# An expert block on one core: the second half of w_down as split products, too

## What is computed

```python
gates = route(h, w_router, router_bias)            # 8 of 64 experts for each token
def per_seq(args):
    hs, gs = args
    g = jnp.einsum('sd,edf->sef', hs, w_gate)      # d = 1024, f = 256
    u = jnp.einsum('sd,edf->sef', hs, w_up)
    act = jax.nn.silu(g) * u * gs[:, :, None]
    return jnp.einsum('sef,efd->sd', act, w_down)  # the down product
```

## Time and profile before

| | us |
|---|---|
| median of 3 runs | 1070.29 |
| lowest, highest | 1069.88, 1074.86 |
| the profiled execution, device time | 1075.07 |
| the profiled execution, span of the instructions | 1073.0 |

### The profile page before, as it was taken

How to read it: one execution, slowest core, us unless ns; L and a number is a source line. 1 busy time by engine, 2 the same in 40 slices (tenths; PEclk the granted TensorE clock), 3 DMA queues, 4 the chain that set the end, 5 groups by cost and what they waited for, 6 DMA issues and landing times.

```text
span 1073.0 us, 15239 instructions
## 1 busy us (share of the span) xinstructions
PE 1019.2 (95%) x4652; PEld 743.2 (69%) x4652; DVE 870.5 (81%) x1416; ACT 644.7 (60%) x743; POOL 299.5 (28%) x224
## 2 busy tenths in 40 slices
PE   4998999999998999999999999999999999999957
PEld 0786776557754777777777777777777777777723
DVE  1669766654768899999998989999999999999785
ACT  5334135643343678777777767777777777777511
POOL 1232221440303433323322323322322332332200
PEclk9899999999999999999999999999999999999979
DMA  9667743112254799999999999999999999999993
GB/s 338 260 244 266 257 174 99 59 40 89 102 212 145 283 376 367 365 378 386 391 382 378 355 365 359 378 374 383 371 373 343 362 335 336 346 358 359 360 412 119
DMA packets 71080, 318.67 MB, mean 297 GB/s; under 512 B 17232, under 2 KB 17744, under 8 KB 44560
## 3 DMA queue, kind: packets, MB, share of 16 engines
q1 hardware_dynamic: 36816, 200.30, 49.3%
q10 hardware_dynamic: 11616, 72.66, 17.9%
q0 software_dynamic: 22624, 45.40, 11.4%
HBM read 317.25 MB, written 39.85 MB: 333 GB/s over the span
## 4 chain that ended last, share of the span: by engine, by line
PE 80%; DMA 9%; DVE 7%; ACT 2%; issue 1%; ACTq 0%; SPq 0%; POOL 0%; DVEq 0%; POOLq 0%
PE ps L1348 11%; PE ps L1350 11%; PE ps L1349 11%; PE ps L1366 10%; PE ps L1033 8%; PE ps L1372 8%; PE ps L1123 6%; DMA hg<-h_rows,idxg 6%; PE ps L1442 3%; PE ps L1225 2%; DMA yr<-y_rows 2%; PE ps L1207 2%; PE ps L1049 2%; PE ps L1174 1%; PE ps L1285 1%
## 5 line engine op out<-in xcount | busy, mean ns | idle before, releaser
L1821 DVE TENSOR_TENSOR wlo<-raw,whi 128x2048 fp32r<-128x2048 f32 x136 | 305.2, 2285 | 0.0
L891 ACT ACTIVATE whi<-raw 128x2048 fp32r<-128x2048 f32 x136 | 261.4, 1923 | 0.0
L1348 PE MATMUL ps<-whi,hthi 128*128 128x512 f32 x544 | 225.1, 414 | 0.0
L1350 PE MATMUL ps<-whi,htlo 128*128 128x512 f32 x544 | 213.8, 393 | 0.0
L1349 PE MATMUL ps<-wlo,hthi 128*128 128x512 f32 x544 | 212.5, 391 | 0.0
L661 POOL DMA_INDIRECT y_rows<-ysb,idxs x68 | 69.0, 1015 | 444.9 <-DVE idxg L1816 389.6
L934 ACT ACTIVATE ysb<-ps 128x1024 f32<-128x1024 f32 x68 | 69.6, 1024 | 175.4 <-PE ps L1372 175.4
L653 POOL DMA_INDIRECT hg<-h_rows,idxg x70 | 140.3, 2005 | 71.0 <-DVE idxg L1816 50.5
L1366 PE MATMUL ps<-rawd,actt 128*128 128x512 f32 x272 | 127.8, 592 | 2.2 <-ACT actt L927 2.2
L1350 PEld LDWEIGHTS ps<-whi,htlo 128*128 128x128 f32 x544 | 102.1, 188 | 23.0
L1349 PEld LDWEIGHTS ps<-wlo,hthi 128*128 128x128 f32 x544 | 102.9, 189 | 17.6
(11 more groups left out here) (272 smaller groups left out, 1611.7 us busy)
## 6 DMA issues: line engine op xcount, KB each, us to landing
raw<-in_w_gate_dram SPq DMA_DIRECT2D x68, 1024.0 KB, 10.9
raw<-in_w_up_dram SPq DMA_DIRECT2D x68, 1024.0 KB, 12.9
rawd<-in_w_down_dram ACTq DMA_DIRECT2D x66, 1024.0 KB, 10.1
ada<-in_w_ada_dram SPq DMA_DIRECT2D x24, 1024.0 KB, 8.3
yr<-y_rows SPq DMA_DIRECT2D x6, 2048.0 KB, 19.3
wraw<-in_w_in_dram POOLq DMA_DIRECT2D x8, 1024.0 KB, 5.7
woraw<-in_w_out_dram SPq DMA_DIRECT2D x16, 256.0 KB, 3.0
yr<-y_rows SPq DMA_DIRECT2D x8, 512.0 KB, 11.7
```

Source lines behind the costliest of these rows:

```text
L891: A(whi[:, s, m_, :], raw[:, s, m_, :], ACT.Copy).then_inc(hi_ok, 1)
L1348: mm(out_, hthi[s][:, k, :], hi, start=(k == 0), stop=False)
L1350: ins = mm(out_, htlo[s][:, k, :], hi, start=False, stop=(k == KD - 1))
L1821: V.tensor_tensor(wlo[s][:, m_, :], raw[:, s, m_, :], whi[:, s, m_, :].bitcast(F32), ALU.subtract).then_inc(lo_dve, 1)
```

## The change

The second half of the down product is split like the first. ScalarE copies the high parts of both halves, one after the other, VectorE makes both low parts, and TensorE computes both halves by three float32r products. `wdhi` now has one buffer for each half in place of one for each slot, so each block uses both. TensorE waits for `actl` and the first low part ahead of the whole down product, and no longer for `actt` and the load. `actt` is still made, since `actl` is computed from it. The one-hot rows stay on VectorE, as before. At the end, `y_out` of the last block but one moves ahead of `down_high` of the last.

```diff
             def down_high(i, s):
                 ac.wait_ge(wd_in[s], i * 16 + 16)
-                A(wdhi[s][:, :, :], rawd[:, s, :, 0:DC], ACT.Copy).then_inc(wdhi_ok, 1)
+                for hf in range(2):
+                    A(wdhi[hf][:, :, :], rawd[:, s, :, hf * DC:(hf + 1) * DC], ACT.Copy).then_inc(wdhi_ok, 1)
...
             silu(last, 1)
+            y_out(last, 0)
             down_high(last, 1)
-            y_out(last, 0)
             act_rows(last, 1)
             y_out(last, 1)
...
             def down(i, s):
-                pe.wait_ge(wd_in[s], i * 16 + 16)
-                pe.wait_ge(actt_ok, num(i, s) + 1)
+                pe.wait_ge(actl_ok, num(i, s) + 1)
                 if not (isinstance(i, int) and num(i, s) == 0):
                     pe.wait_ge(y_ok, num(i, s))
-                for k in range(KF):
-                    mm(bank(5), actt[:, k, :], rawd[:, s, k, DC:D], start=(k == 0), stop=(k == KF - 1))
-                pe.wait_ge(wdlo_ok, num(i, s) + 1)
-                pe.wait_ge(actl_ok, num(i, s) + 1)
-                for k in range(KF):
-                    for j, (a_, w) in enumerate(((acth, wdhi[s][:, k, :]), (acth, wdlo[:, s, k, 0:DC]),
-                                                 (actl, wdhi[s][:, k, :]))):
-                        ins = mm(bank(4), a_[:, k, :], w, start=(k == 0 and j == 0), stop=(k == KF - 1 and j == 2))
+                for hf in range(2):
+                    pe.wait_ge(wdlo_ok, num(i, s) * 2 + (hf + 1))
+                    for k in range(KF):
+                        hi, lo = wdhi[hf][:, k, :], wdlo[:, s, k, hf * DC:(hf + 1) * DC]
+                        mm(bank(4 + hf), acth[:, k, :], hi, start=(k == 0), stop=False)
+                        mm(bank(4 + hf), acth[:, k, :], lo, start=False, stop=False)
+                        ins = mm(bank(4 + hf), actl[:, k, :], hi, start=False, stop=(k == KF - 1))
                 ins.then_inc(dn_mm, 1)
...
             def down_low(i, s):
-                v.wait_ge(wdhi_ok, num(i, s) + 1)
-                V.tensor_tensor(wdlo[:, s, :, 0:DC], rawd[:, s, :, 0:DC], wdhi[s][:, :, :].bitcast(F32), ALU.subtract)\
-                 .then_inc(wdlo_ok, 1)
+                for hf in range(2):
+                    cols = slice(hf * DC, (hf + 1) * DC)
+                    v.wait_ge(wdhi_ok, num(i, s) * 2 + (hf + 1))
+                    V.tensor_tensor(wdlo[:, s, :, cols], rawd[:, s, :, cols], wdhi[hf][:, :, :].bitcast(F32),
+                                    ALU.subtract).then_inc(wdlo_ok, 1)
```

## The result

The changed kernel takes 1077.55 us (median of 12 runs, 1074.26 to 1083.32), the kernel before, on the same chips, 1070.88 us (12 runs, 1068.10 to 1074.86). The ratio is 1.0065, with a 95% interval from 1.0047 to 1.0083: slower by 6.7 us, where the prediction had 35.9 us.

What follows compares the result with a forecast made beforehand. TensorE bounds the kernel at 9.935 us a period; VectorE's chain, 10.48 after the change, was to take over. 65 x (10.48 - 9.935) = +35.4, tail +1.0, start -0.5: +35.9, so 1106 us, range 1095 to 1122.

Steps and rivals of the forecast that it cites:

- TensorE's part: Down product, each period: six split passes (1.40 us) replace four fp32 passes (1.72), saving 0.32; TensorE's period becomes 9.59 us.
- VectorE's added step: One more 128x1024 subtract on VectorE each period, costing 1.13 us with nothing to hide it.
- rival 3: Expert phase: the subtract is absorbed and TensorE stays the bound; 9.59 us a period, -21 us, 1049; chance 0.03.
- VectorE's own chain: VectorE's work per period before the change, two shown waits taken off: 9.35 us, becoming 10.48 with the subtract.
- Rival 2: VectorE's small gaps also close, packing it to busy time: 10.17 us a period, +15 us, 1086; chance 0.09.
- ScalarE's added copy: One more 128x1024 copy on ScalarE each period, 1.06 us, covered by its waiting ahead of `ysb`: cost 0.
- The tail: After the last w_down load: added copies and subtracts before the last down product, +1.0 us, bounds 0 and 2.3.
- Rival 1: Expert phase: TensorE and VectorE take turns and VectorE's old waits stay; 11.07 us a period, +73 us, 1144; chance 0.13.
- Rival 4: Expert phase: TensorE, idle about 0.9 us a period, loses its clock; one period in ten at 1.2 GHz, +57, 1163; chance 0.02.

Runs made afterwards that it cites:

- no_second_low: Changed kernel without VectorE's second subtract; TensorE multiplies the second half's high part twice, omitting its low part: 1075.31 us, ratio 1.0053 to the kernel before.

## Why the prediction was right and wrong

**TensorE's part** was right: six more split passes for four fp32 ones; its own work fell from 9.91 to about 9.54 (from the load at 710.51 to the next ready at 720.15 in the rows above, less 0.10 of waiting for `actl`), and its waits moved to `actl` and the second `wlo`, as forecast.

**VectorE's added step** was right at 1.13 us (1.14), and so was rival 3's rejection: nothing hides it, and a third one costs the same again.

**The failed term is VectorE's own chain**, taken as 9.35 us and worth 8.9. I took the two waits shown in the earlier trace rows off the period and called the rest work. Idle time is counted from the end of the instruction before, but an instruction with nothing to wait for starts before that end: `vcur` 0.09 us before the end of `wdlo` in the earlier trace rows, `actl` 0.09 before the end of the one-hot rows in the changed kernel. A wait shorter than that overlap can't show at all, and a longer one is shown short. The chain held three such waits: `actl` for `acth` (0.29), `slotv` for the indices (0.11), `htlo` for `hthi` (0.03 to 0.05). The 0.29 went unseen in three parts: 0.09 of overlap, 0.15 by which the fourth one-hot record was longer, and the 0.05 from its end (705.23 + 0.89) to 706.17, to which the profile gives no mark. That largest wait stood in my own rows: ScalarE ends `acth` at 706.14 and VectorE starts `actl` at 706.17. I used the 706.14 to argue that `acth` would not be late, and did not compare it with the 706.17. 0.44 us in 65 periods is 29 us, and that is the error of the sum: 35.9 - 28.6 = 7.3, measured 6.7. Rival 2 had the right sign for another reason (closing the gaps in which VectorE reads its own results back); those stayed, as `slotv` to `destr`, 0.31 us, shows. Nor was its 10.17 us a floor: the period came out at 10.04. The busy time of 9.04 contained the longer record of the fourth one-hot instruction (0.15 us), and with the waits gone records overlap that did not before (0.13 us at `slotv`, 0.09 at `actl`). So my sign for rival 2, a period under 10.3, would have named it wrongly.

**ScalarE's added copy at cost 0** was true only beside a VectorE that is as late. `no_second_low` shows it: with VectorE relieved the period is 9.98, not 9.59, and VectorE waits for `acth`, behind that copy. What the copy costs by itself was not measured. I had looked at ScalarE's share and at its one deadline. The loop that it closes spans two blocks: down product, `ysb`, `hthi`, the copies, `acth`, `actl`, both low parts, and back to TensorE. Added up from the rows of `no_second_low` it is 9.9 us a block, and a share of 82% does not show that. For the same reason rival 3 was priced wrong: had VectorE kept up, the kernel would not have gained 21 us, but still have lost between 5 and 6 (the ratio of `no_second_low`, 1.0053).

**The tail** was forecast at +1.0 (0 to 2.3) and came out at 6.0 - 5.1 = +0.9. That was luck, since neither part was foreseen. TensorE, before and after:

```profile
1020.78 0.69 PE L1366 MATMUL ps<-rawd,actt 128*128 128x512 f32 x1 [2.17 <-ACT actt L927]
...
1026.54 0.79 PE L1369 MATMUL ps<-wdhi,acth 128*128 128x512 f32 x1 [6.06 <-DVE actl L1851]
```

The wait ahead of the last down product grew by 3.9 us. The new order gave 1.1 of them (`y_out` waits for TensorE until 1020.30, so the copies of w_down start 10.75 us after the 66th `ysb`, before 9.69 us), where I had put at most 0.4. The added subtract gave another 1.1. The last 1.7 come from TensorE needing `actl` where it had needed only `actt`, which my sum of the tail left out. After this wait the clock was lower: the granted clock was 1.00 in 1009 to 1020.5 us and 0.50, the level of 1.2 GHz, in 1026.5 to 1032. The 12 last passes started 0.43 us apart in place of 0.23, 2.4 us in all; less the 0.3 that the split passes save, that makes the 6.0. The read of the last ranks was then issued 8.6 us later than the earlier trace rows shows, but landed in 6.8 us, median, in place of 11.7. How much of this is cover and how much chance was not tried.

**Rival 1** did not occur, for the reason given: TensorE was ready 0.34 to 0.40 us before VectorE. **Rival 4** did not occur in the 65 periods (granted clock 1.00); only the last down product ran at the lower level.

## What to carry to other kernels

To know what an engine's own chain is worth, compare each start with the end of what it waits for; the idle times of a profile leave out short waits (here up to 0.29 us), and a few of them per period decide whether an added step costs 0.1 or 0.5 us. Before counting on a gain of the engine that sets the pace, add up the other loops around it, over as many blocks as they span: here, once the change was in, TensorE's 9.5 to 9.6 us had ScalarE's 9.8 to 9.9 and VectorE's 10.03 beside it, and the gathered rows close by, so taking 0.32 off TensorE gave nothing. And put a share of work on a neighbouring engine only after looking at what that engine can lock.

## What was not expected of the hardware

A GpSimd subtract of 1.31 us held up a VectorE copy of 0.17 us until it was done, 1.73 us in all, in 59 of 64 blocks. A fourth one-hot instruction beside a gather was recorded 0.15 us longer without delaying the next one. An added VectorE subtract of 1.22 us costs 1.11 to 1.14 us of the period.
